# Expert rows turned by ScalarE and VectorE instead of TensorE, and first-expert rows accumulated into the residual

## The reference, cut to what matters

```python
# hierarchical routing: top-1 of 4 groups, then top-2 of 8 experts in it -> 2 experts a token
order = jnp.argsort(flat_e)              # 8448 assignments, by expert
padded = (counts + 127) // 128 * 128     # each expert's list padded to blocks of 128
def run_block(args):                     # one block: 128 tokens, one expert
    toks, e = args
    xb = h_pad[toks]
    return (silu(xb @ w_gate[e]) * (xb @ w_up[e])) @ w_down[e]
ys = ys * slot_w[:, None]
out = zeros.at[slot_tok].add(ys)         # each token gets the sum of its two experts
x = x + out;  y = rms_norm(x, final_norm_g)
```

## Time and profile before

| what | us |
|---|---|
| three runs: median, lowest, highest | 2895.73, 2894.87, 2897.98 |
| span of the profiled execution | 2897.5 |
| PE busy in it | 2851.8 (98%) |
| DVE, POOL, ACT busy in it | 1575.9, 871.3, 816.7 |
| phase 2, first row transpose to end of the last product | 1960.1 to 2881.4 |

### The profile page before, as it was taken

The page is one execution under the profiler, slowest core; times in us unless marked ns, Lnnn a source line. Parts: engine busy times, 40 slices in busy tenths (PEclk is TensorE's granted clock), DMA queues, the critical chain, the costliest instruction groups (busy, mean ns, idle before and its releaser), DMA issues.

```text
span 2897.5 us, 38361 instructions
## 1 busy us (share of the span) xinstructions
PE 2851.8 (98%) x12809; PEld 1883.5 (65%) x12809; DVE 1575.9 (54%) x4155; ACT 816.7 (28%) x1550; POOL 871.3 (30%) x1366
## 2 busy tenths in 40 slices
PE   8999999999999999999999999979999999999997
PEld 6776777777767767776777677744444444444443
DVE  5656565556555565556565656563444444444444
ACT  2223232322332232323232323222222222222222
POOL 1021111112111211121112111114656665665665
PEclk9999999999999999999999999989999999999999
DMA  7312121211122111211121211267675667567653
GB/s 308 141 52 72 60 74 52 73 70 63 52 73 76 56 59 66 81 52 59 66 81 52 73 59 66 75 224 266 235 267 186 227 202 253 200 222 274 237 171 124
DMA packets 109623, 369.01 MB, mean 127 GB/s; under 512 B 39497, under 2 KB 41426, under 8 KB 99442
## 3 DMA queue, kind: packets, MB, share of 16 engines
q1 hardware_dynamic: 48946, 252.91, 23.9%
q0 software_dynamic: 60480, 113.57, 11.9%
HBM read 325.09 MB, written 140.33 MB: 161 GB/s over the span
## 4 chain that ended last, share of the span: by engine, by line
PE 97%; DMA 1%; DVE 0%; issue 0%; ACT 0%; SPq 0%; POOL 0%; POOLq 0%; DVEq 0%; ACTq 0%
PE PB L368 24%; PE PB L1591 19%; PE PB L379 16%; PE PB L463 12%; PE SS L1631 9%; PE YB L463 4%; PE TB L1576 2%; PE YB L417 2%; PE TB L357 1%; DMA arena<-in_w_in 1%; PE SS L426 1%; PE TB L440 1%; PE SS L430 1%; PE TB L404 1%; PE YB L1624 1%; PE MB L408 1%
## 5 line engine op out<-in xcount | busy, mean ns | idle before, releaser
L368 PE MATMUL PB<-arena,hT 128*128 128x512 f32 (+2 forms) x2112 | 726.8, 497 | 1.7 <-DVE arena L1118 0.9
L368 PEld LDWEIGHTS PB<-arena,hT 128*128 128x128 f32 x2112 | 397.9, 191 | 270.5 <-issue 222.7
L1591 PE MATMUL PB<-arena,hT 128*128 x1296 | 569.3, 592 | 0.0
L379 PE MATMUL PB<-hT,arena 128*128 128x128 f32 x4224 | 487.2, 276 | 4.4 <-DVE arena L1106 4.4
L379 PEld LDWEIGHTS PB<-hT,arena 128*128 128x128 f32 x4224 | 481.8, 193 | 8.2 <-issue 4.6
L1591 PEld LDWEIGHTS PB<-arena,hT 128*128 128x128 f32 x1296 | 246.1, 190 | 309.8 <-issue 309.8
L1143 POOL TENSOR_SCALAR rs<-sq 128x2 f32<-128x2 f32 (+1 forms) x66 | 14.2, 215 | 1304.2 <-ACT h L735 958.0
L463 PE MATMUL PB<-arena,tT 128*128 128x274 f32 (+1 forms) x1056 | 357.8, 493 | 0.7 <-ACT tT L639 0.7
L1631 PE MATMUL SS<-arena,xdt 128*128 x640 | 287.9, 592 | 0.0
L463 PEld LDWEIGHTS PB<-arena,tT 128*128 128x128 f32 x1056 | 195.5, 190 | 140.8 <-issue 120.5
L808 DVE SCALAR_TENSOR_TENSOR xc<-xT,cols,xc 128x128 f32<-128x128 f32 x792 | 216.8, 347 | 3.5
(11 more groups left out here) (273 smaller groups left out, 3585.7 us busy)
## 6 DMA issues: line engine op xcount, KB each, us to landing
arena<-in_w_expert SPq DMA_DIRECT2D x32, 2048.0 KB
arena<-in_w_expert SPq DMA_DIRECT2D x32, 1024.0 KB
h_rows<-h SPq DMA_DIRECT2D x34, 512.0 KB, 2.7
x_in<-in_x_rows SPq DMA_DIRECT2D x33, 512.0 KB, 4.6
hT<-in_x_cols SPq DMA_DIRECT2D x33, 512.0 KB, 3.7
x_res<-in_x_rows SPq DMA_DIRECT2D x33, 512.0 KB, 5.1
dec<-running_sums SPq DMA_DIRECT2D x33, 512.0 KB, 3.7
first_rows<-bc SPq DMA_DIRECT2D x33, 512.0 KB, 3.9
```

What stands on the lines that cost most here:

```text
L368: mm = nc.tensor.matmul(out, hT[u][:, k, :], w_group(name)[:, k, :], start=k == 0, stop=k == KD - 1)
L379: mm = nc.tensor.matmul(PB[b][:, c * P:(c + 1) * P], w_block(name, c)[:, k, :], hT[u][:, k, :], start=k == 0, stop=k == KD - 1)
L1591: mm = nc.tensor.matmul(PB[u][:, :], hT[u][:, k, :], arena[:, bass.ds(slot + k * 2 * DE, 2 * DE)], start=k == 0, stop=k == KD - 1)
```

## The change

- The PE transposes of expert rows go (but for blocks 0 and 1). Instead ACT copies twelve pieces of 32 partitions by 256 elements from the gathered buffer to other partitions (`move`, three of the four groups of 32 tokens), and DVE transposes 32x32 squares (`turn`): one instruction over 512 elements a partition (`zz`), one over 256 (`btok`), and four on 32 partitions straight from the gathered buffer for the fourth group. Together they leave `hT` as before.
- `zz` and `btok`, the pieces' home, have one copy: `move(b)` waits for `pieces_read`, which the first two transposes of `turn(b - 1)` raise.
- The first expert's rows are no longer kept in `first_rows`: the scatter adds them to x2 in DRAM (`keep`, with `compute_op=ALU.add`). Rows that are not a first expert's go to 128 spare rows behind x2, so that all 128 rows are written; five small DVE operations on the list prepare that. `residual(b)` now waits for the scatter of b-1, and one gather (`earlier`) and one DVE addition a block are gone. Phase 1 no longer fills `first_rows`.
- The down product alternates between two PSUM bank pairs, `y_buf` has two buffers instead of four, and all steps are written in a new order. PE's: half of gate/up of b+1, hidden transposes of b, the other half, down of b. POOL's: `keep(b-1)`, `store(b-2)`, `gather(b+4)`, `residual(b)`, root of b-1.

```diff
-        x2_d = nc.dram_tensor("x2_rows", [T, D], F32).ap()
+        x2_d = nc.dram_tensor("x2_rows", [T + P, D], F32).ap()
...
+        moved = [zz[:, 0:DE], zz[:, DE:2 * DE], btok[:, :]]
+        def quarter(b, g, q):
+            return g_buf[b % GB][32 * g:32 * (g + 1), :].rearrange("p (c q i) -> p q c i", q=4, i=32)[:, q, :, :]
+        dn_bank = [[SS[:, n, :] for n in range(2)], [flat(TB[n]) for n in range(2)]]
...
-        y_buf = [x_res[0][:, :], x_res[1][:, :], flat(tT[:, :, :]), flat(wsT[:, :, :])]
+        y_buf = [x_res[0][:, :], x_res[1][:, :]]
...
+            rest, over = lng_b[:, 2 * P:3 * P], lnb_b[:, 3 * P:4 * P]
+            st.link(V.tensor_copy(rest, first_i))
+            st.link(V.tensor_scalar(over, rest, float(T), None, ALU.is_ge))
+            st.link(V.tensor_scalar(rest, rest, float(T), None, ALU.min))
+            st.link(V.scalar_tensor_tensor(out=rest, in0=over, scalar=tok0, in1=rest, op0=ALU.mult, op1=ALU.add))
+            V.tensor_copy(first_i, rest).then_inc(s["idx_out"], 1)
...
+                after(pool, s["gx_T"], 2 * (min(of, 1) + 1))
+                after(pool, s["rows_turned"], of - 1)
...
             def residual(b):
+                after(pool, first_kept, 16 * b)
                 after(pool, s["x2_added"], b - 1)
                 rows_of(x2_d[:, :], xr_buf[b % 2], last_i, b, x2_back[b % 2])
-            def earlier(b):
-                after(pool, first_kept, 16 * b)
-                after(pool, s["first_added"], b - 1)
-                rows_of(first_d[:, :], m_buf[b % 2], last_i, b, first_back[b % 2])
-            def store(b):
-                rows_to(y_out, f_buf[b % 2], last_i, b, y_stored[b % 2])
+            def keep(b):
+                for k in range(2):
+                    pool.wait_ge(s[f"dn_out{k}"], b + 1)
+                nc.gpsimd.indirect_dma_start(out=x2_d[:, :], in_=y_buf[b % 2], in_offset=None, bounds_check=T + P - 1, oob_is_err=True,
+                                             compute_op=ALU.add,
+                                             out_offset=bass.IndirectOffsetOnAxis(ap=first_i[:, b:b + 1], axis=0)).then_inc(first_kept, 16)
...
             def step(b):
-                gather(b + AHEAD)
+                if b > 0:
+                    keep(b - 1)
+                if b > 1:
+                    pool.wait_ge(s["fin_out"], b - 1)
+                    store(b - 2)
+                gather(b + GB)
+                residual(b)
                 if b > 0:
                     pool.wait_ge(s["fin_sq"], b)
                     root_of(1 - b % 2, b)
...
-                for k in range(2):
-                    pool.wait_ge(s[f"dn_out{k}"], b + 1)
-                rows_to(first_d[:, :], y_buf[b % GB], first_i, b, first_kept)
-                residual(b + 1)
-                if b > 0:
-                    pool.wait_ge(s["fin_out"], b)
-                    store(b - 1)
-                earlier(b + 1)
...
-        def pe_gate_up(pe, b, weights=None):
+        def pe_gate_up(pe, b, weights, k0, k1):
             u = b % 2
-            slot, loads = weights or pe_weights(pe, b)
-            pe.wait_ge(w_loaded, loads)
-            for k in range(2):
-                pe.wait_ge(s[f"gx_out{k}"], b + 1)
-            after(pe, s["hb_ready"], b - 1)
-            for k in range(KD):
+            slot, loads = weights
+            if k0 == 0:
+                pe.wait_ge(w_loaded, loads)
+                if b < 2:
+                    for k in range(2):
+                        pe.wait_ge(s[f"gx_out{k}"], b + 1)
+                after(pe, s["rows_turned"], b - 1)
+                after(pe, s["hb_ready"], b - 1)
+            for k in range(k0, k1):
                 mm = nc.tensor.matmul(PB[u][:, :], hT[u][:, k, :], arena[:, bass.ds(slot + k * 2 * DE, 2 * DE)],
                                       start=k == 0, stop=k == KD - 1)
-            mm.then_inc(s["gu_full"], 1)
+            if k1 == KD:
+                mm.then_inc(s["gu_full"], 1)
...
-                u = b % 2
-                pe_gate_up(pe, b + 1)
+                weights = pe_weights(pe, b + 1)
                 slot = entry(pe, TAB_SLOT, b, 0, SLOT_AT[2])
-                pe.wait_ge(s["hb_ready"], b + 1)
-                after(pe, s["hbT_out"], b)
-                for k in range(2):
-                    mm = nc.tensor.transpose(YBv[:, k, :], hb2[u][:, k * P:(k + 1) * P], ident)
-                mm.then_inc(s["hbT_full"], 1)
-                pe_rows(pe, b + 2)
-                pe.wait_ge(s["hbT_out"], b + 1)
-                for n in range(2):
-                    after(pe, s[f"dn_out{n}"], b)
-                    for k in range(2):
-                        mm = nc.tensor.matmul(SS[:, n, :], hTb[:, k, :],
-                                              arena[:, bass.ds(slot + KD * 2 * DE + k * D + n * 512, 512)],
-                                              start=k == 0, stop=k == 1)
-                mm.then_inc(s["dn_full"], 1)
+                pe_gate_up(pe, b + 1, weights, 0, 4)
+                pe_hidden(pe, b)
+                pe_gate_up(pe, b + 1, weights, 4, KD)
+                pe_down(pe, b, slot)
...
+            def move(b, n0, n1):
+                if n0 == 0:
+                    act.wait_ge(gathered[b % GB], 16 * (b // GB + 1))
+                    after(act, s["pieces_read"], b - 2)
+                for n in range(n0, n1):
+                    g, q = n // 4, n % 4
+                    ins = nc.scalar.activation(moved[g][32 * q:32 * (q + 1), :], quarter(b, g, q), ACT.Copy)
+                if n1 == 12:
+                    ins.then_inc(s["rows_moved"], 1)
...
+            def weigh(b):
+                act.wait_ge(s["dn_full"], b + 2)
+                after(act, first_kept, 16 * (b - 1))
+                after(act, s["x2_added"], b - 1)
+                nc.scalar.activation(y_buf[b % 2][:, 0:512], dn_bank[b % 2][0], ACT.Copy, scale=wt[:, b:b + 1]).then_inc(s["dn_out0"], 1)
+            def step(b):
+                hidden(b)
+                move(b + 3, 0, 12)
                 silu(b + 1)
-                rows0(b + 2)
                 if b > 0:
                     squares(b - 1, b)
-                act.wait_ge(s["dn_full"], b + 2)
-                after(act, first_kept, 16 * (b - GB + 1))
-                after(act, s["x2_added"], b - GB + 1)
-                nc.scalar.activation(y_buf[b % GB][:, 0:512], SS[:, 0, :], ACT.Copy, scale=wt[:, b:b + 1]).then_inc(s["dn_out0"], 1)
-            def squares(b, added):
-                act.wait_ge(s["first_added"], added)
-                nc.scalar.activation(h2[:, :], f_buf[b % 2], ACT.Square, accum_out=sq[:, b % 2:b % 2 + 1]).then_inc(s["fin_sq"], 1)
+                weigh(b)
...
+            def turn(b):
+                dve.wait_ge(s["gu_full"], b)
+                dve.wait_ge(s["rows_moved"], b - 1)
+                V.transpose(hT[b % 2][:, :, 0:64].rearrange("p c (g t) -> p g c t", g=2),
+                            zz[:, :].rearrange("p (g c i) -> p g c i", g=2, i=32))
+                V.transpose(hT[b % 2][:, :, 64:96], btok[:, :].rearrange("p (c i) -> p c i", i=32)).then_inc(s["pieces_read"], 1)
+                for q in range(4):
+                    ins = V.transpose(hT[b % 2][32 * q:32 * (q + 1), :, 96:128], quarter(b, 3, q))
+                ins.then_inc(s["rows_turned"], 1)
...
+            def add_x2(u, n):
+                for k in range(2):
+                    dve.wait_ge(s[f"dn_out{k}"], n[0])
+                dve.wait_ge(x2_back[u], n[1])
+                if n[2] is not None:
+                    after(dve, y_stored[u], n[2])
+                V.tensor_tensor(f_buf[u], y_buf[u], xr_buf[u], ALU.add).then_inc(s["x2_added"], 1)
             def step(b):
-                u = b % 2
+                turn(b + 2)
+                gate(b + 1)
                 if b > 0:
-                    dve.wait_ge(s["x2_added"], b)
-                    add_first(1 - u, 16 * (b // 2))
-                gate(b + 1)
-                rows1(b + 2)
-                dve.wait_ge(s["dn_full"], b + 2)
-                after(dve, first_kept, 16 * (b - GB + 1))
-                V.tensor_scalar(y_buf[b % GB][:, 512:], SS[:, 1, :], wt[:, b:b + 1], None, ALU.mult).then_inc(s["dn_out1"], 1)
+                    add_x2(1 - b % 2, (b, 16 * ((b + 1) // 2), 16 * ((b - 1) // 2)))
+                weigh(b)
+                if b % 2 and b // 2 >= SURE - 1:
+                    V.tensor_copy(final_i, last_i[:, b - 1:b + 1])
                 if b > 0:
-                    norm(1 - u, b)
-                for k in range(2):
-                    dve.wait_ge(s[f"dn_out{k}"], b + 1)
-                dve.wait_ge(x2_back[u], 16 * (b // 2 + 1))
-                after(dve, y_stored[u], 16 * (b // 2))
-                V.tensor_tensor(f_buf[u], y_buf[b % GB], xr_buf[u], ALU.add).then_inc(s["x2_added"], 1)
-                if b % 2 and b // 2 >= SURE - 1:
-                    V.tensor_copy(final_i, last_i[:, b:b + 1])
+                    norm(1 - b % 2, b)
```

94 lines of the change are left out of this document (55 added, 39 removed).

## The result

The changed kernel takes 3019.97 us (median of four runs, 3014.12 to 3023.74) against 2896.79 of the kernel before beside it: 1.042 times as long (95% interval 1.0410 to 1.0435). I had forecast 2827, with 2820 to 2885 as the range. The profiled execution has a span of 3014.7 us.

| what | before | after |
|---|---|---|
| PE busy in the span, us | 2851.8 (98%) | 2843.1 (94%) |
| period of a step in phase 2, us | 11.40 | 12.9 to 13.0 |
| ACT busy in the span, us | 816.7 | 1180.3 |

The account below looks back on a forecast made before the run. PE was taken to bound phase 2. The profiled 2897.5 us, less 69.6 for row transposes, plus 1.0 between the phases, gave 2828.9, or 2827 for the median; range 2820 to 2885.

Parts of the forecast that it names:

- PE's frame: Phase 2 on PE: row transposes leave, a step falls from 11.40 to 10.53 us, saving 69.6 us over 80 steps.
- Loop one: Through the pieces' home on ACT, DVE and POOL: moves to transposes in series, 10.16 us, 0.37 below PE's 10.53.
- Rival A: Moves and transposes loop longer than PE's work: 2852 us, or 2861 to 2900 with dearer transposes; chance 0.20.
- rival D: Nothing won: another loop turns in about 11.4 us, such as moves 0.41 apart giving 11.36 and 2894; chance 0.05.
- Loop two: POOL's in-order loop through the accumulating scatter: 4.24 us + L, taken as 9.7 against PE's 10.53.
- L: Time from the end of issuing keep to its landing: taken as 5.5 us, possible ends 3.2 and 9.5.
- rival C: Slower than before: POOL's residual waits for the previous keep, mean L from 7.16 us; 2963 at 8; chance 0.13.
- B: Rival: scatter slow but not ruinous, mean L of 6.5 to 7.2 us, +57 us, 2884; chance 0.12.
- The DMA sum: All DMA transfers of a step: rows 6.1 us plus weights 3.2, 9.3 of 10.53, fitting with little room.
- only a mean above 6.3: POOL's scatter loop: PE is stopped only if the mean L exceeds 6.3 us.
- a single late one does not stop PE: One late scatter leaves PE unheld, since the hidden product is ready some 5 us ahead.
- Between the phases and the end: Five more DVE operations between phases cost +1.0 us of at most 1.4; the run's end 0, within 1.5.

Follow-up runs that it names:

- e7: Changed kernel with two homes for the pieces and, from the fifth expert on, weight loads of only 1 KB a partition (wrong weights): 2831.3 us.
- e4: Changed kernel with ACT's twelve moves in five forms (partitions and run lengths varied, rows partly wrong); run once, 2995.0 us, no comparison in time.
- e11: Changed kernel with its one home for the pieces and, from the fifth expert on, weight loads of 1 KB a partition (wrong weights): 2913.0 us.
- e12: e2 with keep dropping the rows that are not a first expert's, and without the five list operations: 2911.4 us.
- e2: Changed kernel with a second home for the pieces, in a free buffer, so moves wait one block less strictly: 2983.6 us.
- e10: e2 with the same weight bytes loaded in DMAs of 2 KB a partition instead of 16 and 8 KB: 2905.0 us.
- e14: Changed kernel with two homes, rows dropped, 2 KB loads, root before residual, and POOL's gather ahead of keep: 2869.9 us.
- e8: Changed kernel with two homes, a plain scatter of first experts' rows instead of accumulation, its readers a block later, silu after the eighth move: 2994.2 us.

## Why the prediction was wrong, step by step

- *PE's frame, 10.53 us and 69.6 less.* Right: e7's step is 10.52 and its time 2831.3 against 2827 forecast. Turning on ACT and DVE costs PE nothing, and cutting gate/up in halves costs nothing either.
- *Loop one, 10.16.* Failed in one term. Twelve moves are 12 x 0.425 = 5.1 instead of 3.72. The other terms, 6.44, came out as summed: 10.16 + 1.38 = 11.54 against 11.57 measured, the transposes within 0.03 of my 1.09. The row I took the 0.31 from the earlier trace rows has 128 partitions, the same ones for source and result. e4 shows that neither the 32 partitions nor the short runs end the overlap: 0.72 for two copies in a row on the same partitions, 0.84 for two that go from one group of partitions to others. Rival A had the right loop with 0.35 a move, and rival D had nearly the right distance (0.41) with a loop of 11.36, "no change". Alone it costs 82 us (e11 less e7), and would have made the kernel 0.5% slower than before.
- *Loop two, 4.24 + L.* Failed in L and in its split. With hardly any loads (e7) the way is 7.77, against my 7.56. This agreement is in part luck: the issue is 2.33 instead of 1.26, and L, which I had at 5.5, is 7.77 - 0.8 - 2.33 = 4.6. So 128 rows read twice were not priced too low: the plain rows take 159 ns and the added ones some 328, about half the rate. That is the rule of the Trainium skill that the prediction drew on (Collectives: The Full Stack, "The bandwidth ceiling: the fold count and why AG ≠ RS ≠ AR"), and for a scatter with addition the trace agrees. The issue of 2.47 instead of 1.26 is a term of its own, since a keep whose issue was 0.74 shorter landed 0.79 earlier (e7). The prediction knew that a DVE operation beside an issue doubles it and left it out of its 4.24; here the norm lies beside keep's issue in nearly every step. What I had dismissed was the collision: "the weight load that caught that scatter comes once in two and a half blocks". An expert has two loads, issued at different times and landing 9.4 and 5.7 us after their issue, and 39 of 54 keeps met one. Fewer rows suffer less from it (8.04 in e12), and the mean grows by 2.6 to 10.37. The loop is 10.37 + 2.18 = 12.55 (root 0.28 + 0.57, gap 0.23, residual and gap 1.1), against a step of 13.04; I did not take the other 0.5 apart. This is the outcome of rival C: in the prediction's terms L was 10.37 - 0.8 - 2.47 = 7.1, at C's point of 7.16, and the issue, 1.2 longer than priced, took it beyond. But C's reason for it, rows at three times the price of a plain one, was not the cause; the collision, which stood under B as a thing against it, was. Alone loop two costs 152 us (e2 less e7), of which fewer rows give back 72 (e12) or smaller packets 79 (e10).
- *The DMA sum, 9.3 of 10.53, "with little room".* Its size was right (0.725 x 13.04 = 9.5 us a step), but it was no measure. e7's DMA engines are at 62% (59.3 + 3.0), the changed kernel's at 72.5, and the first is not late at all; e10's are at 82.2 (51.4 + 30.8, 2100 to 2700) and its scatter is less late than the changed kernel's. What counts is how long a single transfer is held.
- *The two loops together.* e11's and e2's losses, 82 and 152, sum to 234; the whole is 3020.0 - 2831.3 = 189. They overlap in part: what one loop waits, the other need not wait again. I had treated the loops as alternatives, each against PE, with "only a mean above 6.3" of L as danger. e12 shows that this is wrong as well: its mean way of 8.04 gives a loop of 10.2, under 10.53, and still the step is 11.56. My reading is that with a spread of several us late steps are lost and early ones not won, against the prediction's "a single late one does not stop PE"; no run tests this by itself.
- *Between the phases and the end.* In e7 both lie inside its 4 us above the forecast. The end was not 0, as I had it within 1.5: from the end of PE's last product to the end of the span there are 16.1 us before, 18.8 in e7 and 23.7 in the changed kernel.

What stays open: what exactly ends the overlap of ACT's copies, how rows and weight packets take turns on a DMA engine, and why e14's runs lie 33 us apart. A version without accumulation in a good order was not tried beyond e8.

## What to carry to other kernels

A sum of durations tells that a loop fits only if each row has the same shape and the same partitions as the new instruction, and stands behind a like one: 12 moves at 0.11 us too little were enough to lose the gain. An in-order wait for a DMA's landing should be priced at the slow end of landings while the largest loads are in the queues, not with the mean, and against the slack of one step. Before such a wait is accepted, cut the loads into smaller pieces, drop rows instead of writing them to a spare place, and put what does not need the landing beside it.

## What the runs showed of the hardware

- ACT copies of 256 elements that follow each other onto different partitions do not overlap (0.425 us from start to start); on the same partitions they do (0.31 to 0.32), at 32 or 128 partitions and in short or long runs alike (e4).
- DVE's float32 transposes took 0.70 us for 512 elements a partition, 0.40 for 256, and stood 0.45 apart on 32 partitions (four in 1.79).
- In the changed kernel an accumulating scatter of 128 rows that met weight packets in its first 6 us took 11.36 us to the start of what waited for it, one that met none 8.00 (39 and 15 cases).
- With the same bytes of weights, loads in DMAs of 2 KB a partition instead of 16 and 8 KB shortened the mean way of an accumulating scatter from 10.42 to 9.07 us and the kernel by 79 us.
- The issue of the accumulating scatter of 128 rows took 2.54 us with DVE's norm (a SCALAR_TENSOR_TENSOR of 1024 elements) beside it and 1.64 without, with transposes beside it both times (50 and 3 cases in the changed kernel); in e7 the shorter issue landed 0.79 us earlier.
